# Four norms folded into their routers, with token-major statistics and without filler products

## What is computed

```
# layers 0, 1 (i)
x = x + g1 * mix
h = rmsnorm(x, norm_g[i, 1]) * (1.0 + sc2) + sh2
x = x + g2 * hier_moe(h, ...)        # logits = h @ w_group, h @ w_expert; top 2 of 32 experts per token

# layers 2, 3 (i)
x = layer_norm(ALPHA * x + mix @ w_o[i], ln1_g[i], ln1_b[i])
ffn = expert_choice_moe(x, router_w[i], ...)   # 16 experts, each takes its top 32 tokens by softmax affinity
ple = sigmoid(x @ ple_gate_w[i] + ple_gate_b[i]) * (p[i] @ ple_w[i])
x = layer_norm(ALPHA * x + ffn + ple, ln2_g[i], ln2_b[i])
```

## Time and profile before

| | |
|---|---|
| median of three runs | 2262.51 us |
| lowest and highest | 2256.45 and 2264.46 us |
| profiled execution, its own time | 2256.44 us |
| profiled execution, span | 2254.7 us |
| PE busy | 1823.6 us, 81% of the span |
| DVE, ACT busy | 426.8 us and 374.3 us |
| granted PE clock, mean | 0.893 of full |
| loaded by DMA | 716.06 MB, mean 318 GB/s |

### The profile page before, as it was taken

One profiled execution on the slowest core, in us unless ns is written; L12 is line 12 of the kernel. 1 busy time (PEld: TensorE's weight loads), 2 busy tenths in 40 slices (PEclk: granted clock), 3 DMA queues, 4 the chain that ended last, 5 costly groups with the idle time before them and its releaser, 6 DMA issues.

```text
span 2254.7 us, 30726 instructions
## 1 busy us (share of the span) xinstructions
PE 1823.6 (81%) x13207; PEld 1135.9 (50%) x13207; DVE 426.8 (19%) x973; ACT 374.3 (17%) x796; POOL 0.6 (0%) x5
## 2 busy tenths in 40 slices
PE   7989988999899989899988556655889976566565
PEld 5868655667576656587854121211567642222113
DVE  2242211123533111124311000000243210000001
ACT  3131211112523111123211000000223210000001
POOL 0000000000000000000000000000000000000000
PEclk9999999999899999999998787787999987877868
DMA  9876799885536999943479999999933699999994
GB/s 359 251 256 239 323 392 397 354 247 203 210 133 255 358 395 394 318 147 130 150 305 415 422 421 421 421 422 421 329 131 114 264 413 422 421 421 422 421 421 166
DMA packets 184047, 716.06 MB, mean 318 GB/s; under 512 B 27709, under 2 KB 95209, under 8 KB 113385
## 3 DMA queue, kind: packets, MB, share of 16 engines
q1 hardware_dynamic: 183196, 713.57, 81.1%
q10 hardware_dynamic: 716, 0.53, 0.1%
HBM read 826.25 MB, written 1.05 MB: 367 GB/s over the span
## 4 chain that ended last, share of the span: by engine, by line
PE 55%; DMA 33%; DVE 4%; SPq 3%; ACT 2%; issue 2%; ACTq 0%; POOLq 0%; DVEq 0%
DMA ring<-in_w 27%; PE ps L950 19%; PE ps L1357 7%; DMA ring<-in_moe_w_up 6%; PE ps L1280 5%; PE ps L1266 2%; PE ps L1290 2%; PE ps L1369 2%; PE ps L1307 2%; PE ps L1060 2%; PE ps L929 2%; PE ps L1017 2%; SPq L777 1%; PE ps L964 1%; SPq L836 1%
## 5 line engine op out<-in xcount | busy, mean ns | idle before, releaser
L1357 PE MATMUL ps<-ring,ptb 128*32 128x512 f32 x1936 | 325.0, 823 | 200.4 <-DMA ring<-in_w 187.0
L1357 PEld LDWEIGHTS ps<-ring,ptb 128*32 128x32 f32 x1936 | 84.7, 145 | 427.7 <-issue 412.9
L1369 PE MATMUL ps<-ring,pb 128*32 128x512 f32 x1024 | 146.4, 726 | 88.2 <-DMA ring<-in_w 85.6
L950 PE MATMUL ps<-xT,ring 128*128 128x256 f32 (+2 forms) x640 | 146.0, 387 | 1.0 <-ACT xT L1663 0.3
L1369 PEld LDWEIGHTS ps<-ring,pb 128*32 128x32 f32 x1024 | 39.9, 130 | 188.7 <-issue 184.5
L950 PEld LDWEIGHTS ps<-xT,ring 128*128 128x128 f32 (+2 forms) x640 | 117.3, 186 | 29.4 <-issue 8.7
L950 PE MATMUL ps<-oT,ring 128*128 128x256 f32 x512 | 112.8, 380 | 2.4 <-DVE oT L2036 1.4
L2309 DVE TENSOR_TENSOR kT<-pb,ps 128x1024 f32<-128x1024 f32 x8 | 9.8, 1221 | 550.9 <-ACT pb L1817 550.9
L1280 PE MATMUL ps<-ring,yT 128*32 128x256 f32 x1536 | 92.8, 400 | 19.0 <-DMA ring<-in_moe_w_up 16.7
L950 PE MATMUL ps<-hT,ring 128*128 128x256 f32 x480 | 106.7, 380 | 1.5 <-ACT hT L1663 1.5
L950 PEld LDWEIGHTS ps<-oT,ring 128*128 128x128 f32 x512 | 97.0, 190 | 16.5 <-DVE oT L2088 2.0
(11 more groups left out here) (412 smaller groups left out, 1939.0 us busy)
## 6 DMA issues: line engine op xcount, KB each, us to landing
ring<-in_w SPq DMA_DIRECT2D x370, 1024.0 KB
ring<-in_moe_w_gate SPq DMA_DIRECT2D x96, 1024.0 KB
ring<-in_moe_w_up SPq DMA_DIRECT2D x96, 1024.0 KB
ring<-in_moe_w_down SPq DMA_DIRECT2D x96, 1024.0 KB
ring<-in_ada_w SPq DMA_DIRECT2D x48, 1024.0 KB
ring<-in_diff_w_in SPq DMA_DIRECT2D x12, 1024.0 KB
ring<-in_w_o SPq DMA_DIRECT2D x8, 1024.0 KB
ring<-in_ple_gate_w SPq DMA_DIRECT2D x8, 1024.0 KB
```

The costliest lines, as they stand in the source:

```text
L950: last = mmul(o, l, r, start=start, stop=stop)
L1357: last = mmul(ps[32 * j:32 * j + 32, 2 * a + h, :], xg[:, k, 32 * j:32 * j + 32], w[j][2 * k2 + h], start=(k == 0), stop=(k == C - 1))
L1369: last = mmul(ps[32 * j:32 * j + 32, 6 + h, :], hidT2[:, c, 32 * j:32 * j + 32], w[j][2 * c2 + h], start=(c == 0), stop=(c == C - 1))
```

## The change

`FOLDED = (1, 3, 5, 7)`: these norms are no longer carried out before the router.

- The sums `xT` are transposed to tokens while the output products still run (`turn_pair`), unnormalised. DVE takes mean and variance of each token from PSUM with `bn_stats` and `bn_aggr` (`half_moments`, `deviation`), ACT takes the root, DVE the reciprocal: `rstd` and `away` are columns of 128 tokens.
- The gain is multiplied into the router's weights (`router_weights`), the shift becomes a row (`router_rows`), and the logits come from products with raw `xT` pairs, which DVE scales by `rstd` and adds to the row (`logits`). For layers 2 and 3 the rows are made in group 0 of the first expert stage: 32 products of 128x16 on PE, then eight DVE operations.
- ACT's copy of the tokens scales them by `rstd`; the gain and shift are applied to the gathered tokens, four ACT operations where one copy was (`gathered`).
- In layers 2 and 3 `xT` itself is normalised after the dispatch (`normalise_x`), beside the expert products.
- Modulation piece 4 moves from the router of layer 0 to the first attention, whose steps are now 0, 1, 2, 3, 5; pieces 5 and 9 are spread over the selection.
- All `idle_products` are gone. Three small loads are added to `load_late` and one wait of SP names `tok_mm`. Several semaphores share names.

```diff
-ADA_STEP = {"diff": (0, 2, 4, 5), "nsa": (1, 5, 9)}
+ADA_STEP = {"diff": (0, 1, 2, 3, 5), "nsa": (1, 5, 9)}
-ADA_ROUTER = {0: (4, 5), 1: (9,)}
+ADA_ROUTER = {0: 5, 1: 9}
...
-                sp.wait_ge(S("sq_mm"), 6 + 2 * l)
+                sp.wait_ge(S("tok_mm"), 2 * (2 + l) + 1)
                 load_guests(range(5, 7))
...
-                project(fill[1:2])
-                if n >= 2 and n != 3:
-                    idle_products(7, 4 if fill else 8)
+            def turn_pair(n, a):
+
+                pe.wait_ge(S(x_pair(n, a)[0]), x_pair(n, a)[1])
+                for tt in range(TT):
+                    for c in (2 * a, 2 * a + 1):
+                        last = tr(ps[:, tok_bank(tt) + c // 4, P * (c % 4):P * (c % 4) + P], xT[:, c, P * tt:P * tt + P])
+                if a % 2:
+                    last.then_inc(S("tok_mm"), 1)
...
+            def norm_router(n, out, fill=()):
+
+                m = n // 2
+                for a in range(4):
+                    project([span[out][a]])
+                    if n < 5 and a == 0:
+                        pe.wait_ge(S("late_params"), 16 * N_LATE)
+                        pe.wait_ge(S("mod_ready"), m + 1)
+                        router_rows(m, 128)
+                    elif a:
+                        turn_pair(n, a - 1)
+                        logits(m, a - 1)
+                turn_pair(n, 3)
+                logits(m, 3)
+                project(fill[0:2])
...
                         last.then_inc(S("lr_mm"), 1)
+                        if m == 0:
+                            router_rows(2, 0)
+                            router_rows(3, 64)
...
+                    if i == 0:
+                        for tt in range(TT):
+                            for a, x in enumerate((rstd, away)):
+                                last = mmul(ps[:, 7, T * a + P * tt:T * a + P * tt + P],
+                                            x[:, tt:tt + 1].to_broadcast([P, P]), ident, start=True, stop=True)
+                        last.then_inc(S("rstd_mm"), 1)
...
+            def root(m):
+
+                func(misc[:, 54:55], eps_col, ACT.Sqrt)
+                act.wait_ge(S("max_ready"), 2 * m + 1)
+                func(rstd, mean_var[:, :, 1], ACT.Sqrt, bias=eps_col).then_inc(S("sum_ready"), 1)
+                func(misc[:, 57:58], eps_col, ACT.Exp)
...
                     act.wait_ge(S("e1_xg_mm"), x0 + at + 1)
-                    half = at % 2
-                    func(xpair[at // 2 % 2][:, 4 * half:4 * half + 4, :].rearrange("p k s -> p (k s)"), psf(bank, 2),
-                         ACT.Copy).then_inc(S("e1_xg_ready"), 1)
+                    for c in range(4):
+                        k = 4 * (at % 2) + c
+                        by, add = gathered_gain(m, k)
+                        last = func(xpair[at // 2 % 2][:, k, :], ps[:, bank + c // 2, T * (c % 2):T * (c % 2) + T],
+                                    ACT.Identity, scale=by, bias=add)
+                    last.then_inc(S("e1_xg_ready"), 1)
...
+            def deviation(m):
+
+                link(half_moments(m, 1))
+                for tt in range(TT):
+                    last = V.bn_aggr(mean_var[:, tt, :], moments[:, tt, :, :].rearrange("p h s -> p (h s)"))
...
                 dispatch1(1)
+                if m == 0:
+                    router_weights(2, 0)
+                    router_weights(3, 64)
                 dve.wait_ge(S("lr_ready"), m + 1)
                 combine1(0)
```

More of the change, by code:

```diff
@@ L493, in ple_gate_jobs @@
                 job(A["ple_gate_w_2"][layer][:, 256 * s:256 * s + 256], 8, 256,
-                    mm_T(xT, 8, [(0, P, 0, 0), (P, P, 0, T)]), ev, bank=GATE_BANK)
+                    mm_T(xT, 8, [(0, P, 0, 0), (P, P, 0, T)]), ev, bank=GATE_BANK,
+                    need=("h_ready", 6 + 2 * layer) if s == 0 else None)
         GATE_AT = (16, 24, 32, 32)
@@ L565, in tok_bank, with scaled, plain @@
             return 2 + 4 * tt
+        FOLDED = (1, 3, 5, 7)
+        def scaled(n):
+            return n - (n > 1) - (n > 3)
+        def plain(n):
+            return n - sum(x < n for x in FOLDED)
         def h_chunk(n, k):
             if k < GAIN_ACT:
-                return "h_ready", GAIN_ACT * n + k + 1
-            return "h_rest", (C - GAIN_ACT) * n + k - GAIN_ACT + 1
+                return "h_ready", GAIN_ACT * scaled(n) + k + 1
+            return "h_rest", (C - GAIN_ACT) * scaled(n) + k - GAIN_ACT + 1
         def await_norm(eng, n):
@@ L943, in project @@
                         await_need(pe, ("job", j - 2))
+                    if chunked and jb["bank"] == GATE_BANK:
+                        pe.wait_ge(S("xn_ready"), 4 * scaled(jb["need"][1]))
                     for x, grp in enumerate(jb["mm"](slot_view(jb["slot"], jb["k"], jb["cols"]), jb["bank"])):
@@ L1215, in route1 @@
                 rank_of(sel, E1, m).then_inc(S("rank_mm"), 1)
[L1216 to L1217 removed]
+                ada_part(*ada, range(4, 6))
                 pe.wait_ge(S("nblk_ready"), m + 1)
@@ L1664, in gain, with norm @@
                     last.then_inc(S("h_ready"), 1)
-            def norm(n, fill=()):
-                roots(n, fill)
+            def norm(n):
+                squares(n)
+                std(n)
                 gain(n)
@@ L1806, in gathered @@
                         act.wait_ge(S("xg_mm"), 2 * n - 1 + h)
-                        func(xf[:, 512 * h:512 * h + 512], ps[:, 4 + h, :], ACT.Copy).then_inc(S("xg_ready"), 1)
+                        for c in range(4):
+                            by, add = gathered_gain(m, 4 * h + c)
+                            last = func(xg[:, 4 * h + c, :], ps[:, 4 + h, P * c:P * c + P], ACT.Identity,
+                                        scale=by, bias=add)
+                        last.then_inc(S("xg_ready"), 1)
                 gathered(E2_GROUPS * l + 1)
@@ L1986, in scale, with normalise_x, half_moments @@
                     ins.then_inc(S("xn_ready"), 1)
+            def normalise_x(n):
+                dve.wait_ge(S("rstd_mm"), n // 2 - 1)
+                for ins in pairs(xT, ps[:, 7, 0:T], ALU.mult):
+                    last = ins
+                link(last)
+                for ins in pairs(xT, ps[:, 7, T:2 * T], ALU.add):
+                    ins.then_inc(S("xn_ready"), 1)
+                gain(n)
+                await_norm(dve, n)
+            def half_moments(m, h):
+                dve.wait_ge(S("tok_mm"), 2 * m + h + 1)
+                for tt in range(TT):
+                    last = V.bn_stats(moments[:, tt, h, :], ps[:, tok_bank(tt) + h, :])
+                return last
@@ L2452, in _ @@
             ada_vectors(0, 2, 4, psf(2, 2), 2)
+            ada_vectors(1, 0, 1, ps[:, 4, 0:T], 2)
             modulation(1)
-            V.memset(misc[:, 55:56], 0.0).then_inc(S("gain_ready"), 1)
-            residual("diff_out", gate=0)
-            norm(1)
+            spread_chunks(1)
+            residual("diff_out", 0, gate=0)
             route1(0)
@@ L2508, in _ @@
             modulation(3)
-            residual("nsa_out", gate=1)
-            norm(3)
+            spread_chunks(3)
+            residual("nsa_out", 1, gate=1)
             route1(1)
```

297 lines of the change are left out of this document (173 added, 124 removed).

## The result

The changed kernel takes 2272.78 us (median of 20 runs, 2264.42 to 2281.32), the kernel before 2263.1 us (20 runs, 2256.45 to 2270.89): a ratio of 1.0039, 95% interval 1.0027 to 1.0051, or +9.7 us: slower by 0.4%, with an interval that leaves out 1. The prediction was 2270 us, +9.6, "no change, leaning slow". Its sum was right; single terms were not, and they made up for each other.

A forecast was written before the change was run, and what follows sets the result against it. Loads were taken to bound the expert stages of layers 2 and 3, mostly PE's program elsewhere. Terms 5.5 - 4.3 - 0.8 - 10.4 + 9.5 + 0.8 + 4.5 + 3.4 + 1.4 = +9.6 us, giving 2270 us, range 2253 to 2283.

The forecast's parts named there:

- First attention, +5.5: First attention: with a modulation piece in every step, three steps of 7.4 us and one of 3.8; bounds +2.3 and +6.2.
- Layer 0, -4.3: Layer 0, last output product to gather: 9.3 us to the selection against 13.6; the removed piece needs no further gain.
- Layer 1, -0.8: Layer 1, last output product to gather: -1.4 us from the folded norm, less 0.6 for piece 9 inside the selection.
- Layers 2 and 3, -5.2 each: Before the expert streams: -7.2 us to the gather, +1.0 broadcast products, +1.0 clock; all of it reaches the end.
- Group 0, +9.5: Layer 0's experts: 32 more products and DVE's work delay the hidden rows, nothing absorbed; bounds +4.7 and +11 us.
- Gathered copies, +0.8: Gathered tokens: four operations for one copy add 0.8 us for layers 0 and 1, hidden elsewhere.
- Clock at norms 2, 4 and 6, +4.5: Without fillers each projection behind these norms begins at half clock, 1.5 us each; bounds 0 and 1.7 each.
- At the gathers, +3.4: Layers 0 and 1: their gathers follow idle time and start at slow clock, +3.4 us together.
- Rows in layers 0 and 1, +1.4: The rows may bring a slow stretch in the next output product, at four in ten; bounds 0 and 3.4 us.
- Slow clock among the output products: Rival, chance 0.22: two slow stretches in each layer's output stage, +21.8 us in all, 2282 us.
- Gain not passed on: Rival, chance 0.05: another load sets the start of the expert streams, so the 10.4 us are lost, 2280 us.
- Delays absorbed: Rival, chance 0.15: layer 0's experts hide group 0's delay, attention its piece, no slow stretch appears; -12.4 us, 2248 us.

The follow-up runs named there:

- the run with the piece alone: The kernel before with only modulation piece 4 moved from layer 0's router into the first attention: 2265.74 us, ratio 1.0017 to the kernel before.
- The run with fillers: The changed kernel with eight filler products again behind the sums of norms 2, 4 and 6: 2265.51 us, ratio 1.0020 to the kernel before.
- the one with norm 4 alone: The changed kernel with eight filler products behind the sums of norm 4 only: 2269.18 us, ratio 1.0033 to the kernel before.
- with the waits filled: The changed kernel with rows at norms 2 and 6, piece 4 in layer 0's selection, fillers or piece 9 in other waits: 2247.2 us, ratio 0.9932 to before.

## Why the prediction was right, by its own terms

- **First attention, +5.5.** The steps came out as computed, 7.4 us each, +6.2 over the four (the last step, 4.55, had a further wait of 0.67; the upper bound). The stage grew by 8.2: besides the steps, more of it ran at half clock (0.89 on the mean, 0.94 before), and the clock terms had nothing there. In the two profiles with the same five pieces and a mean clock of 0.94 the stage takes 60.3 and 60.8 us. That is an undersized term.
- **Layer 0, -4.3.** The selection starts 4.85 us after the last output product (5.4 was stated). Rows 2.4 us instead of 3.1, `bn_stats` 0.65 instead of 0.68. From diff_out to the gather -4.6 and -4.8, but 2.6 of that (54.45 to 51.84 in the run with the piece alone) comes from the piece that left, which the step "it lay beside the norm" had at nothing; so the folded norm alone gave about 2 there. The gather, which a slow stretch met, took it back: to gate/up the changed kernel needs 59.9 and 58.3 us, the run with the piece alone 58.8.
- **Layer 1, -0.8**, with the rows' clock 0: -0.5 to the gather, and the selection starts 5.1 us after the last output product. Right, but up to gate/up the fold gives nothing in layers 0 and 1 (layer 1: 59.7 and 59.2 us, 58.0 before), since PE waits for DVE again (4.11 and 4.35 us) and then runs slowly.
- **Layers 2 and 3, -5.2 each.** -6.2 to -6.7 and -8.3. The mechanism held, the size was 1.0 to 1.5 too small in layer 2: from the first output product to the gather it is 46.6 us for 54.5, 7.9 less where 7.2 was counted. "PE is the later one" held up to the affinities; then DVE's selection was the path, with 2.93 and 0.98 us of waiting. Layer 3 gained more because before had a slow value product there (3.61 us).
- **Group 0, +9.5.** +10.9 and +9.1, and the two runs that move the rows out and double their products show that all of it reached the end. The bounds held. By the two profiles the new products held DVE up for 10.1 and 8.3 us, where 7.8 and 0.3 for the clock were counted, and DVE's own part took 3.5 in place of 4.1.
- **Gathered copies, +0.8.** +0.4 and +0.4. Right.
- **Clock at norms 2, 4 and 6, +4.5.** The run with fillers puts it at 6.7, the one with norm 4 alone puts that norm's part at 2 to 3. The error is the step "half speed for some 3.4 us ... which costs 1.7": one such stretch is indeed lost in the nsa projection (+0.5 to +1.4), but the even mixer lost 5.0 (its mean clock fell from 0.96 to 0.92) and the odd one 2.3 (0.95 to 0.93), so more than one stretch can follow, in the even mixer above all. **At the gathers, +3.4:** +3.0 or +1.6, and +2.3 or +1.7. Right, up to one place. **Rows in layers 0 and 1, +1.4:** nothing; both output stages have clock 1.00.
- **The rivals.** "Slow clock among the output products" did not occur: 1.00 over 33 us in layer 0, and 1.00 in the output stages of the other three layers too. "Gain not passed on" did not: the first freed slot moved 7.1 us nearer, and the stages behind it kept their length. "Delays absorbed" did not: DMA's share was 0.02.
- **The page's rule.** That "the default state is throttled, and activity releases the throttle" (the Trainium skill, "TensorE: Matmul & The Clock Gate", "What's actually happening") fits the nsa projection at 0.58, and the projections behind norms 2, 4 and 6 in all runs: wherever eight fillers fill the wait, 16 places in all, they start at a clock of 1.00. But "the trace agrees wherever a wait is long" said too much. Two long waits of the kernel before, the first of them the one from which the 1.7 us come:

```profile
289.69 5.21 PE L1280 MATMUL ps<-ring,yT 128*32 128x256 f32 x64 [3.90 <-DMA ring<-in_moe_w_up]
...
1250.66 3.64 PE L1357 MATMUL ps<-ring,ptb 128*32 128x512 f32 x32 [3.95 <-DMA ring<-in_w]
```

The second wait is as long, and what follows it has a clock of 1.00 (1250.7 to 1254.3). The rule doesn't tell where slow stretches fall inside a stage that is dense throughout: with more products in group 0 PE is busy for 16.00 of 16.00 us at a mean clock of 0.66.

The terms of the sum that were too small on the slow side (attention 2.7, even mixer 3.5) and on the fast side (layers 2 and 3, 1.0 to 3.1 each) and the 1.4 that did not come cancel. The mechanisms were right in the main; that the sum met the measured 9.7 within 0.1 us is luck.

## What to carry to other kernels

A change that removes a wait should be costed together with what fills the waits that remain: here the folded norms took 14 to 15 us out of layers 2 and 3 (18 with the waits filled), and it was given back by work put at three bad places, an attention whose steps already had a wait, a group on which the DMA of a whole stage hangs, and bare waits ahead of dense work. Ask of every small piece of constant work which stage has time for it: the same 16 products and DVE's operations cost half of 9 to 11 us in group 0 and nothing where DMA bounds. Filler products were worth 6.7 us ahead of three projections, and real work with rows as long as theirs (a modulation piece of 256 columns) fills a wait as well.

## What was not expected of the hardware

- Products of 128x16 in an unbroken row lose the full clock although PE is busy throughout: 1.86, 1.94, 3.36, 3.57 us for four equal sets (1.86, 1.94, 1.94, 3.16 in the second profile), and 0.50 over the last 10 us when there were twice as many.
- As fillers such products are unreliable. Sixteen of them stood in the wait of norm 2, 4 or 6 in seven places of four runs. In two of these, both at norm 2, the projection behind them starts at a clock of 1.00; in the other five at 0.50 to 0.65, twice at norm 2 with the same code. Eight products of 128x256 kept it at 1.00 in 16 places of 16. Of 19 bare waits one (shown above) was followed by full clock, the others by 0.50 to 0.71 over the first 3.4 us of the projection.
- Two profiles of the kernel before agree within 0.5 us in every stage, though its timed runs spread over 17 us and their medians lie 5 to 7 us higher. Two profiles of the changed kernel differ by 6 us, in the expert stages of layers 0 (2.4 us longer in the second) and 1 (3.6 us shorter) above all. A stage read from one profile has to be taken with that in mind; what differs there was not found out.
